# Summing the modulation over partitions: nine column groups move from TensorE's row sums and transposes to VectorE's 32x32 transpose and row sums

## What is computed

```
for i in range(DEPTH):
    mod_l = silu(c) @ ada_w[i] + ada_b[i]          # latent stream, 6 x 1024
    mod_c = silu(c_ctx) @ ada_w[i] + ada_b[i]      # context stream, 6 x 1024
    sh1, s1, g1, sh2, s2, g2 = split(mod_l, 6)
    h = x * (1 + s1) + sh1
    x = LN(alpha * x + g1 * mixer(h))
    x = LN(alpha * x + g2 * (relu((x * (1 + s2) + sh2) @ w1) ** 2 @ w2))
    # and the same for ctx with mod_c, in layer 0
```

## Time and profile before

| | |
|---|---|
| median of 3 runs | 1933.3 us |
| the profiled execution | 1933.96 us, of which span 1932.1 us |
| TensorE (PE) busy | 1921.8 us, 99% |
| VectorE (DVE) busy | 1371.3 us, 71% |
| ScalarE (ACT) busy | 674.7 us, 35% |
| GpSimd (POOL) busy | 381.2 us, 20% |
| granted TensorE clock | 0.999 of 2.4 GHz |

### The profile page before, as it was taken

How to read it: one execution, slowest core, us unless ns; L and a number is a source line. 1 busy time by engine, 2 the same in 40 slices (tenths; PEclk the granted TensorE clock), 3 DMA queues, 4 the chain that set the end, 5 groups by cost and what they waited for, 6 DMA issues and landing times.

```text
span 1932.1 us, 24878 instructions
## 1 busy us (share of the span) xinstructions
PE 1921.8 (99%) x9432; PEld 1653.0 (86%) x9432; DVE 1371.3 (71%) x1977; ACT 674.7 (35%) x936; POOL 381.2 (20%) x364
## 2 busy tenths in 40 slices
PE   9999999999999999999999999999999999999998
PEld 6889899899889988998888888888888888888887
DVE  3756587698887777767887755754764787777778
ACT  2423122145323222331546225324413443434443
POOL 0300312313211222222310130130030037110004
PEclk9999999999999999999999999999999999999999
DMA  9623334345998998898596285366447525977656
GB/s 327 262 70 67 120 121 131 106 135 134 210 230 216 215 230 231 229 236 226 175 223 240 88 251 181 129 192 197 151 144 231 173 90 178 246 210 194 175 146 148
DMA packets 120419, 350.59 MB, mean 181 GB/s; under 512 B 17520, under 2 KB 30448, under 8 KB 115568
## 3 DMA queue, kind: packets, MB, share of 16 engines
q1 hardware_dynamic: 91200, 268.11, 40.9%
q0 software_dynamic: 27280, 77.08, 22.2%
q10 hardware_dynamic: 1824, 3.85, 0.6%
HBM read 296.01 MB, written 40.92 MB: 174 GB/s over the span
## 4 chain that ended last, share of the span: by engine, by line
PE 95%; POOL 1%; DMA 1%; DVE 1%; issue 1%; ACT 0%; SPq 0%; POOLq 0%; DVEq 0%; ACTq 0%
PE bank L1157 18%; PE bank L1159 18%; PE bank L1158 18%; PE bank L1195 4%; PE bank L1196 4%; PE bank L1197 4%; PE bank L1565 3%; PE bank L1564 3%; PE bank L1562 3%; PE bank L1626 3%; PE bank L1627 3%; PE bank L1624 3%; PE bank L1809 2%; PE bank L1808 2%; PE bank L1806 2%; PE bank L1468 1%
## 5 line engine op out<-in xcount | busy, mean ns | idle before, releaser
L2377 DVE TENSOR_TENSOR w_lo<-raw,w_hi 128x1024 fp32r<-128x1024 f32 x132 | 168.8, 1282 | 170.8 <-ACT w_hi L1832 170.6
L1832 ACT ACTIVATE w_hi<-raw 128x1024 fp32r<-128x1024 f32 x132 | 139.2, 1055 | 279.3 <-PE bank L1159 158.9
L1157 PE MATMUL bank<-w_hi,act_hi 128*128 128x512 f32 x504 | 198.2, 393 | 0.0
L1159 PE MATMUL bank<-w_hi,act_lo 128*128 128x512 f32 x504 | 196.4, 390 | 0.0
L1158 PE MATMUL bank<-w_lo,act_hi 128*128 128x512 f32 x504 | 196.3, 390 | 0.0
L1157 PE MATMUL bank<-hT_hi,w_hi 128*128 128x384 f32 (+2 forms) x544 | 191.8, 353 | 0.0
L1158 PE MATMUL bank<-hT_lo,w_hi 128*128 128x384 f32 (+2 forms) x544 | 190.8, 351 | 0.0
L1159 PE MATMUL bank<-hT_hi,w_lo 128*128 128x384 f32 (+2 forms) x544 | 190.8, 351 | 0.0
L1195 PE MATMUL bank<-w_hi,hT_hi 128*128 128x512 f32 x336 | 131.0, 390 | 0.0
L1196 PE MATMUL bank<-w_lo,hT_hi 128*128 128x512 f32 x336 | 130.8, 389 | 0.0
L1197 PE MATMUL bank<-w_hi,hT_lo 128*128 128x512 f32 x336 | 130.7, 389 | 0.0
(11 more groups left out here) (458 smaller groups left out, 4858.2 us busy)
## 6 DMA issues: line engine op xcount, KB each, us to landing
raw<-w_units_d SPq DMA_DIRECT2D x234, 512.0 KB, 4.6
mod<-mod_units_d SPq DMA_DIRECT2D x64, 384.0 KB, 4.5
wsum<-w_units_d SPq DMA_DIRECT2D x44, 512.0 KB, 4.5
raw<-weight_sums_d SPq DMA_DIRECT2D x32, 512.0 KB, 4.4
wsum<-w_units_d POOLq DMA_DIRECT2D x25, 512.0 KB, 7.9
wsum<-wsum POOLq DMA_DIRECT2D x19, 512.0 KB, 7.0
bv<-mod_units_d SPq DMA_DIRECT2D x16, 512.0 KB, 3.6
weight_sums_d<-w_units_d POOLq DMA_DIRECT2D x8, 1024.0 KB, 12.4
```

The source lines that it names most:

```text
L1157: nc.tensor.matmul(out, s_hi, m_hi, start=first, stop=False)
L1159: return nc.tensor.matmul(out, s_lo, m_hi, start=False, stop=last)
L1832: nc.scalar.activation(halves_of(phase, k, i)[0], raw[:, s, :], ACT.Copy).then_inc(hi_done, 1)
L2377: tt(lo, raw[:, s, :], f32(hi), ALU.subtract).then_inc(lo_done, 1)
```

## The change

Each of the nine groups is now summed so. `part_sum` on VectorE transposes the sums in blocks of 32x32 (STREAM_TRANSPOSE), so that the 32 partitions of a quadrant stand in a row, and a TENSOR_REDUCE over every 32 adds them. What is left are four partial sums for each column, one in every quadrant of 32 partitions. `part_columns` on TensorE adds the four with a 128x32 matrix of zeros and ones (`sel32`, made once from the identity by a TENSOR_REDUCE): four matmuls, 16, 12 or 6 columns wide, at the four column positions of the array, which write 32 partitions of bank 7 each. `add_part_bias` adds the bias. The rows, ScalarE's copy of them, the transposes on TensorE and the steps `rows0`, `rows2` of these groups fall away. `gmlpz` and `ffn0z` keep the old form. Semaphore `lg_dve` is renamed `small_done` and counts the new small VectorE steps as well; GpSimd's and SyncE's lists stay the same.

```
+            def part_columns(phase, i, label, n, vectors):                       # TensorE
+                sums = part_sums_v if phase == "vz" else part_sums
+                pe.wait_ge(small_done, sums_made(phase, i))
+                free(phase, i, label)
+                for q in range(4):
+                    src = sums[:, 0:vectors, 0:4 * n].rearrange("p v (j q) -> p q j v", q=4)[:, q]
+                    last = nc.tensor.matmul(bank[7][32 * q:32 * q + 32, 0:n * vectors].rearrange("p (j v) -> p j v", v=vectors),
+                                            sel32[:, :], src, start=True, stop=True, tile_position=(0, 32 * q))
+                last.then_inc(pe_step, 1)
...
-                    (1, 5): sums_2, (2, 5): lambda: mod_columns("vz", 0, 2, rbuf[:, 0, :], 7)})
+                    (2, 5): lambda: part_columns(phase, i, "cols2", 8, 2)})
...
-                    down(phase, i, CH, TILES0, act_hi0, act_lo0, ready, rows=rows, columns=columns)
+                    down(phase, i, CH, TILES0, act_hi0, act_lo0, ready,
+                         columns1=lambda: part_columns(phase, i, "cols0", 8, 2))
...
-                    down(phase, i, 7, TILES0, act_hi0, act_lo0, ready, rows1=rows, columns1=columns)
+                    down(phase, i, 7, TILES0, act_hi0, act_lo0, ready, after=TILES0 - 2,
+                         columns1=lambda: part_columns(phase, i, "cols0", 6, 2 if p < PIECES_MIXED else 1))
...
+            def part_sum(done, v, a, src, turned, sums=part_sums):               # VectorE
+                n = src.shape[1] // 32
+                dve.wait_ge(small_done, done)
+                nc.vector.transpose(turned, src).then_inc(small_done, 1)
+                dve.wait_ge(small_done, done + 1)
+                nc.vector.tensor_reduce(sums[:, v, a:a + n], turned.rearrange("p (n r) -> p n r", r=32),
+                                        mybir.AxisListType.X, ALU.add).then_inc(small_done, 1)
...
+                    group1_sum(p, 0)
+                    group1_sum(p, 1)
                     block0_lo(p + 1, 0)
                     drain0(p, 1, 0)
+                    group1_sum(p, 2)
                     drain0(p, 1, 1)
-                    mod1_columns(phase, i)
+                    group1_sum(p, 3)
                     for t in range(2, TILES0 - 1):
                         drain0(p, 1, t)
                         products(5, t - 2)
+                    add_part_bias(phase, i, "cols0", 1, 6 * i, 6, 2 if p < PIECES_MIXED else 1)
```

More of the change, by code:

```diff
@@ L353, in build @@
         lg = sb("lg", [P, 5, 8])
+        part_sums = bst[:, :, :, :].rearrange("p a b c -> p (a b c)")[:, 0:64].rearrange("p (v n) -> p v n", v=2)
+        sel32 = sb("sel32", [P, 32])
         ADAB, LNC, BU, LNG, LNB = 0, 96, 160, 176, 192
@@ L790, in build, with sums_made @@
         ws_half = [wsT[:, 4 * h:4 * h + 4, :].rearrange("p a b -> p (a b)") for h in range(2)]
+        def sums_made(phase, i):
+            done = 11
+            if phase == "vz":
+                return done
+            if phase == "gmlp":
+                return done + 4 * (i + 1)
+            return done + 4 * (PIECES_A - 2) + 8 * min(i + 1, PIECES_MIXED) + 4 * max(0, i + 1 - PIECES_MIXED)
         block = keep.enter_context(nc.Block())
@@ L1202, in token_units, with down @@
                             between[q, t]()
-            def down(phase, i, k0, tiles, a_hi, a_lo, ready, late=None, rows=None, columns=None, rows1=None, columns1=None):
+            def down(phase, i, k0, tiles, a_hi, a_lo, ready, late=None, columns1=None, after=1):
                 for half in range(2):
@@ L1254, in down @@
                                     last.then_inc(pe_step, 1)
-                                    if t == 1 and columns1:
+                                    if t == after and half == 1 and columns1:
                                         columns1()
@@ L1258, in down @@
                                 last.then_inc(pe_step, 1)
[L1259 to L1262, removed]
             def down_blocks(phase, k0, order, a_hi, a_lo, ready, ln_phase=None, late=None, rows=None, columns=None):
@@ L1567, in ffn0 @@
                         last.then_inc(pe_step, 1)
[L1569 to L1576, removed]
-                def rows():
[L1579 to L1584, removed]
+                def rows():
+                    pe.wait_ge(mod_used, len(MOD1_SEQ))
+                    mod_sums(phase, i, "rows0", 6, [sum1(p), sum1(PIECES_F - 1, 1)], WIDE_M1 // 2)
                 def columns():
-                    if phase == "ffn0" and p >= PIECES_MIXED:
-                        column_sums("cols0", 7, 1)
-                        return
                     mod_columns(phase, i, 0, rows1, 7)
@@ L2633, in ffn0, with down @@
                     split_lo("heads", 0, 1)
-            def down(phase, i, k0, tiles, then=None):
+            def down(phase, i, k0, tiles, then=None, sums=None, columns=None):
                 if phase not in ("heads", "ffn1a"):
@@ L2643, in down @@
                 split_lo(phase, i, k0 + 3)
+                if sums:
+                    sums()
                 if phase == "ffn1a":
@@ L2649, in down @@
                     drain(phase, i, 1, t, tiles)
+                    if t == 1 and columns:
+                        columns()
             C11, C12, Z57, NEG21, NEG16 = range(5)
@@ L2917, in product, with add_part_bias @@
                 last.then_inc(used, 1)
+            def part_sum(done, v, a, src, turned, sums=part_sums):
[5 more added lines that the diff above has]
+                                        mybir.AxisListType.X, ALU.add).then_inc(small_done, 1)
+            def add_part_bias(phase, i, label, layer, c, n, vectors):
+                dve.wait_ge(pe_step, step_of(phase, i, label))
+                src = bank[7][:, 0:n * vectors].rearrange("p (j v) -> p j v", v=vectors)
+                if vectors == 1:
+                    src = src.to_broadcast([P, n, 2])
+                bias = cols[:, ADAB + 48 * layer + c:ADAB + 48 * layer + c + n].unsqueeze(2).to_broadcast([P, n, 2])
+                tt(modc[:, layer, c:c + n, :], src, bias, ALU.add).then_inc(dve_drain, 1)
             def product_v(n):
@@ L2933, in product_g @@
                 elif m:
-                    dve.wait_ge(pe_step, step_of("gmlp", m // KC - 1, "cols0"))
+                    dve.wait_ge(small_done, sums_made("gmlp", m // KC - 1))
                 product(sums_g, units_g[m % SLOTS_G], m % KC, 2, mod0_used)
@@ L2947, in _ @@
                     product_v(4 * n)
+                if n == 2:
+                    dve.wait_ge(mod0_used, KC)
+                    for v in range(2):
+                        part_sum(7 + 2 * v, v, 0, sums_v[v], stage[:, :, :].rearrange("p a b -> p (a b)"), part_sums_v)
                 split_lo(phase, i, 2)
@@ L2968, in _ @@
                 if n == 0:
-                    dve.wait_ge(lg_dve, 5)
+                    dve.wait_ge(small_done, 5)
                     dve.wait_ge(lg_act, 2)
-                    tt(lg[:, 0, :], lg[:, 0, :], lg[:, 3, :], ALU.mult).then_inc(lg_dve, 1)
+                    tt(lg[:, 0, :], lg[:, 0, :], lg[:, 3, :], ALU.mult).then_inc(small_done, 1)
+                    nc.vector.tensor_reduce(sel32[:, :], ident[:, :].rearrange("p (x r) -> p r x", x=4), mybir.AxisListType.X,
+                                            ALU.add).then_inc(small_done, 1)
                 split_lo(phase, i, 4)
@@ L3044, in _, with group_sums, group_columns @@
                 if phase != "gmlpz":
[L3045 to L3049, removed]
+                    def group_sums():
+                        dve.wait_ge(mod0_used, KC * (p + 1))
+                        for v in range(2):
+                            part_sum(sums_made(phase, i) - 4 + 2 * v, v, 0, sums_g[v], stage[:, :, :].rearrange("p a b -> p (a b)"))
+                    def group_columns():
+                        add_part_bias(phase, i, "cols0", 0, 8 * (2 + p), 8, 2)
+                    if p:
+                        down(phase, i, CH, TILES0, lambda: normalise_v(p + 1), group_sums, group_columns)
+                    else:
+                        down(phase, i, CH, TILES0, lambda: normalise_v(p + 1))
                 else:
@@ L3072, in mod_product, with group1_sum @@
                 last.then_inc(mod_used, 1)
+            def group1_sum(p, n):
+                vectors = 2 if p < PIECES_MIXED else 1
+                if n >= 2 * vectors:
+                    return
+                v, half = vectors - 1 - n // 2, n % 2
+                dve.wait_ge(mod_used, MOD1_SEQ.index((p, KC - 1)) + 1)
+                w = WIDE_M1 // 2
+                part_sum(sums_made("ffn0", p) - 4 * vectors + 2 * n, v, half * w // 32, sum1(p, v)[:, half * w:(half + 1) * w],
+                         rows1[:, :])
             def mod1_columns(phase, i):
                 dve.wait_ge(pe_step, step_of(phase, i, "cols0"))
[L3077 to L3090, removed]
```

(3 more changed lines are left out.)

47 lines of the change are left out of this document (20 added, 27 removed).

## The result

The kernel after takes 1940.78 us (median of six runs, 1938.99 to 1941.2) against 1933.07 us before (six runs, 1932.54 to 1934.34): a ratio of 1.0037, 95% interval 1.0024 to 1.0049. The forecast was 1924.3 us, 9.0 us faster; the kernel became 7.7 us slower. What makes it surprising is that nearly everything the forecast had looked at came out as it said. First part 1 of the profile's page and the waits of TensorE, both of the kernel after; they stand against the earlier trace rows.

What follows compares the result with a forecast made beforehand. TensorE's own stream was taken as the bound: 12.75 us of old groups leave, 3.8 of narrow groups come, 9.0 us gained, so 1933.3 - 9.0 = 1924.3 us. The 8-in-10 range was 1922.0 to 1929.5.

Steps and rivals of the forecast that it cites:

- what leaves it is gained in full: All nine places: TensorE's own stream is the time, so work removed from it is saved until another engine is late.
- one short reduction in a gap near the start: Making sel32 on VectorE: a single reduction near the start; no separate time was given for it.
- all nine old groups together: TensorE's loss of old work: 3 x 1.63 + 3 x 1.30 + 6 x 0.66 = 12.75 us.
- the one that ended slower: Rival: slow transpose makes TensorE wait at part_columns in five places; 1947 us at four clocks an element; 3 in 100.
- What bounds the kernel: Whole kernel: TensorE busy 1921.8 of 1932.1 us, four waits of 3.4 us together, none in the middle.
- What TensorE loses and gains: Nine groups: old ones cost 12.75 us, new narrow ones 0.42 each, 3.8 together; balance 9.0 us saved.
- What VectorE gains: New transposes and reductions on VectorE: 1.23 us each at 1024 columns, 0.56 at 384.
- Whether TensorE waits for it: VectorE's new chains fit everywhere without making TensorE wait; gmlp has 0.8 us to spare, mixed pieces 0.5.
- the tightest place: Mixed pieces of the first MLP: VectorE ready at 580.4, TensorE at 580.9, 0.5 us to spare.
- What was to show it wrong: Signs: part_columns waiting 1 us or more for TENSOR_REDUCE, distances of 1.4 us, or 63.2 us pieces with new weight waits.

Runs made afterwards that it cites:

- after_sel_first: Kernel after, with the selection tensor allocated ahead of all others, so all tensors lie 128 bytes higher and none moves against another: 1921.76 us, ratio to before 0.9943.
- the padding: Kernel after, plus an unused tensor of 32 columns behind the selection tensor, so the layers' tensors lie 256 bytes higher than before: 1923.16 us, ratio 0.995.
- before_shift128: Kernel before, plus an unused 32-column tensor where the change allocates its selection tensor; the layers' tensors lie 128 bytes higher: 1949.82 us, ratio 1.0086.
- before_shift64: Kernel before, plus an unused 16-column tensor at the selection tensor's place; the layers' tensors lie 64 bytes higher: 1951.46 us, ratio 1.0095.
- before_shift192: Kernel before, plus an unused 48-column tensor at the selection tensor's place; the layers' tensors lie 192 bytes higher: 1941.3 us, ratio 1.0044.
- before_actlo128: Kernel before, with 32 unused columns ahead of act_lo0 and 32 behind it, so act_lo alone lies 128 bytes off: 1939.9 us, ratio 1.0034.

## Why the prediction was wrong, point by point

- **The step that failed** stands in its first paragraph, and the sum rests on it: "what leaves it is gained in full". That takes the rest of TensorE's stream as unchanged, at 0.228 us a step, and so counts the new operations but not the new allocation. `sel32` was priced as "one short reduction in a gap near the start"; as a reduction it is (0.37 us). As 128 bytes ahead of the layers' tensors it costs 18.0 us in TensorE's steps, more than the 12.75 us at which the prediction put all nine old groups together. No rival had this; the one that ended slower had a slow transpose for its reason.
- **What bounds the kernel**: right. TensorE's waits hold no new line, in the kernel after and in after_sel_first.
- **What TensorE loses and gains**: right in mechanism, a little small. In after_sel_first, laid beside the kernel before by place in the program, the lead grows by 1.29 us at the `vz` group, 1.27 at each `gmlp` group, and by 6.28 over the six groups of the first MLP, 1.05 each: 10.1 us, where 9.0 was forecast. Measured as the prediction did it, to the second plain matmul behind, the old groups come to 12.95 us and the new ones to 3.48, 9.5 in all; the rest of the 10.1 is not told apart by any run. A narrow group costs 0.38 us with 6 columns and 0.39 with 12 and 16, forecast 0.42: the width hardly matters. The Trainium skill (TensorEngine Tiling (Array Packing), Key Properties) has a drain at each change of tiling mode. These numbers agree with it, but they would agree as well with a price of the eight short instructions and their weight loads, which no run separates from it.
- **What VectorE gains**: right. A transpose of 1024 columns takes 1240 ns and its reduction 1220, forecast 1.23 us; at 384 columns 574 and 553, forecast 0.56. The two sizes differ by 666 ns for 640 columns, 1.04 ns a column. The Trainium skill says one element per cycle and lane (Vector Engine (DVE) Microarchitecture Reference, 3.8 The reshape front-end), and the trace agrees: the prediction's estimate from that page, 1.07 us for 1024 columns, is 1.04 ns a column too.
- **Whether TensorE waits for it**: right. In the kernel after, `gmlp` has 293.74 - 292.46 = 1.28 us to spare, forecast 0.8. But there TensorE itself comes later by its slower steps: in after_sel_first, where they are fast, it is 292.35 - 291.53 = 0.82, as forecast (last reduction and narrow group below). The mixed pieces, forecast as the tightest place with 0.5, have 0.97 in that run.

```profile
290.31 1.22 DVE L2930 TENSOR_REDUCE bst<-stage 128x32 f32<-128x1024 f32 x1
...
292.35 0.26 PE L1376 MATMUL bank<-bst,sel 128*32 128x16 f32 x8
```

- **The time**: with the memory laid out as before, the kernel after takes 1921.76 us (1923.16 with the padding) against the forecast of 1924.3. Some of that is the 1.1 us by which the change was undervalued. The rest goes with the opening, and that is luck: it differs by some 2 us from one execution to another, also where nothing of it was changed (at 60 us before_shift128 is 2.0 us ahead of the kernel before, before_shift64 0.4).
- **What was to show it wrong**: pieces of 63.2 us did appear, but were to come with new waits for weights. They came with none. Of the views that the prediction named, only the distance between plain matmuls, which it used as a constant, could have shown the cause.

## What to carry to other kernels

A new tensor is part of a change's price: list which tensors it moves, and compare the distance of each matmul's two operands before and after. Where TensorE is the bound, the step of a plain matmul in code that was not touched is the first number to compare, since a busy engine with no waits hides a loss of 2% in each slow step. A small tensor goes where it moves everything or nothing, or is padded to 256 bytes here; that was worth 17.6 us and more to this kernel (1940.78 - 1923.16), more than the change itself gives.

## What the runs showed of the hardware

- The step of an fp32r matmul of 512 columns depends on where its two operands lie to each other: 226.7 to 227.3 ns at a multiple of 256 bytes, 232.4 to 233.3 at 32, 64 and 128 bytes off, 229.1 at 192 (weights above the stream).
- It is not symmetric. With the stream 192 bytes above the weights (`gw` and `in_scr` as streams, `hT` as weights, before_shift192) the step is 233.0 and 233.3, as with the weights 64 above the stream. With the stream 64 above (before_shift64) `in_scr` steps at 228.9, as with the weights 192 above, but `gw` at 233.3: the distance alone does not give the size.
- With 384 columns and `s` as the stream only the distance of 128 shows (176.1 ns for 173.3); 32, 64 and 192 are free. With `hT` as the stream and `in_s` as the weights 64 costs as well (176.6, before_shift64).
- One misplaced load of weights costs two steps, 5.2 and 6.4 ns (before_actlo128).
- A group of four fp32 matmuls of 32 weight columns between full ones costs 0.38 to 0.39 us of TensorE's time at 6, 12 and 16 columns (after_sel_first).
- VectorE's transpose of fp32 in blocks of 32x32 takes 574 ns at 384 columns and 1240 at 1024, 1.04 ns for each column between (kernel after).
